# Stage borders, an affine step, and joined level pairs in a two-block transformer kernel on one core

## The reference

```python
# first block
h = x + stick_breaking(rms(x)) @ w_o;         h += swiglu(rms(h))
h += dilated(rms(h, mix), rms(h, kv)) @ w_o;  h += swiglu(rms(h));  h = rms(h, final)
# second block
h = layer_norm(ALPHA*h + hgrn2(h));           h = layer_norm(ALPHA*h + conv_ffn(h))
h = layer_norm(ALPHA*h + window(h, k, v));    h = layer_norm(ALPHA*h + conv_ffn(h))
# hgrn2, 8 heads:  S_t = diag(f_t) S_{t-1} + k_t v_t^T ;  o_t = S_t^T q_t
```

## Time and profile before

| | us |
|---|---|
| median of 3 runs (2432.78 to 2435.87) | 2432.88 |
| the profiled execution, its own time | 2434.52 |
| its span, first to last instruction | 2432.7 |
| PE busy | 2401.2 |
| DVE busy | 1430.5 |
| ACT busy | 909.2 |
| POOL busy | 162.3 |

### The profile page before, as it was taken

The page is one execution under the profiler, slowest core; times in us unless marked ns, Lnnn a source line. Parts: engine busy times, 40 slices in busy tenths (PEclk is TensorE's granted clock), DMA queues, the critical chain, the costliest instruction groups (busy, mean ns, idle before and its releaser), DMA issues.

```text
span 2432.7 us, 31033 instructions
## 1 busy us (share of the span) xinstructions
PE 2401.2 (99%) x11450; PEld 1958.9 (81%) x11450; DVE 1430.5 (59%) x2358; ACT 909.2 (37%) x1299; POOL 162.3 (7%) x171
## 2 busy tenths in 40 slices
PE   9999999999999999999989999999999999999998
PEld 7777888888777788888878887888888887888886
DVE  4776645533767555543278886766653766766643
ACT  4454322222756432222233333533321564433312
POOL 0000000000000000000020000000030451000031
PEclk9999999999999999999999999999999999999999
DMA  5122233233222233322231222233223412333232
GB/s 175 61 61 77 91 100 95 86 95 104 61 61 80 79 102 95 95 86 95 92 106 54 69 69 89 86 100 98 86 95 99 135 58 91 96 96 98 82 113 95
DMA packets 61078, 219.45 MB, mean 90 GB/s; under 512 B 6805, under 2 KB 7349, under 8 KB 60864
## 3 DMA queue, kind: packets, MB, share of 16 engines
q1 hardware_dynamic: 58464, 208.28, 27.0%
q0 software_dynamic: 2064, 9.50, 1.1%
q10 hardware_dynamic: 464, 0.48, 0.1%
HBM read 216.12 MB, written 2.12 MB: 90 GB/s over the span
## 4 chain that ended last, share of the span: by engine, by line
PE 93%; DVE 4%; ACT 2%; issue 1%; DMA 0%; DVEq 0%; SPq 0%; ACTq 0%
PE ps L264 26%; PE ps L266 26%; PE ps L265 26%; PE ps L2044 1%; PE ps L1066 1%; PE ps L303 1%; PE ps L304 1%; PE ps L308 1%; PE ps L1054 1%; PE ps L1223 1%; PE ps L1203 1%; PE ps L1080 1%; PE ps L1167 1%; PE ps L1168 1%; PE ps L1173 1%
## 5 line engine op out<-in xcount | busy, mean ns | idle before, releaser
L264 PE MATMUL ps<-xh,wh 128*128 128x512 f32 x1832 | 728.4, 398 | 5.2 <-DVE wl L258 5.2
L266 PE MATMUL ps<-xh,wl 128*128 128x512 f32 x1832 | 713.9, 390 | 0.0
L265 PE MATMUL ps<-xl,wh 128*128 128x512 f32 x1832 | 713.5, 389 | 0.0
L250 ACT ACTIVATE wh<-raw 128x1024 fp32r<-128x1024 f32 x331 | 348.1, 1055 | 509.7 <-PE ps L266 472.8
L258 DVE TENSOR_TENSOR wl<-raw,wh 128x1024 fp32r<-128x1024 f32 x331 | 409.0, 1237 | 203.4 <-ACT wh L250 201.7
L264 PEld LDWEIGHTS ps<-xh,wh 128*128 128x128 f32 x1832 | 344.2, 188 | 80.2 <-DVE wl L258 6.9
L266 PEld LDWEIGHTS ps<-xh,wl 128*128 128x128 f32 x1832 | 344.0, 188 | 72.5
L265 PEld LDWEIGHTS ps<-xl,wh 128*128 128x128 f32 x1832 | 344.4, 188 | 70.3 <-issue 2.2
L431 DVE TENSOR_TENSOR wl<-raw,wh 128x1024 fp32r<-128x1024 f32 x56 | 81.8, 1460 | 217.6 <-ACT wh L428 217.6
L264 PE MATMUL ps<-wh,up_ah 128*128 128x512 f32 x528 | 205.7, 390 | 1.1 <-DVE wl L431 1.1
L266 PE MATMUL ps<-wh,up_al 128*128 128x512 f32 x528 | 205.4, 389 | 0.0
(11 more groups left out here) (305 smaller groups left out, 3313.2 us busy)
## 6 DMA issues: line engine op xcount, KB each, us to landing
raw<-weights SPq DMA_DIRECT2D x387, 512.0 KB, 3.6
cst<-rows_d POOLq DMA_DIRECT2D x9, 512.0 KB, 5.0
hgrn_mask<-levels POOLq DMA_DIRECT2D x1, 2560.0 KB, 9.4
window_bias<-bias_rows POOLq DMA_DIRECT2D x1, 2048.0 KB, 10.1
hT<-x_t SPq DMA_DIRECT2D x7, 256.0 KB, 6.5
out_t<-hT SPq DMA_DIRECT2D x7, 256.0 KB, 2.1
cst<-consts SPq DMA_DIRECT2D x1, 832.0 KB, 9.0
raw<-weights SPq DMA_DIRECT2D x2, 256.0 KB, 4.5
```

Of the source, the lines that this page charges most:

```text
L250: act.activation(wh[slot][:, :], raw[slot][:, :], ACT.Copy).then_inc(hi_done, 1)
L264: pe.matmul(out, w_hi, m_hi, start=first, stop=False, **kw)
L265: pe.matmul(out, w_hi, m_lo, start=False, stop=False, **kw)
L266: return pe.matmul(out, w_lo, m_hi, start=False, stop=last, **kw)
```

## The change

- Recurrence: levels 6 and 7 become a fourth pair with a buffer `W3` and a mask more (11 levels in the mask table). Wide products alternate between two pairs of banks (0-1 and 2-3; in the last head 0-1 and 4-5). Seven products become six, ten picks eleven.
- POOL's gains of the norm behind down1 move from ahead of the recurrence into heads 1 to 4 of its loop, one tile in each, behind that head's root.
- Behind down1: squares of half 0 are taken as soon as that half is added; the second square covers 512 columns, and the root gets the first sum as a bias. DVE adds block b+1 before it normalises block b.
- Layer norms: both halves of the last block are normalised on DVE; tiles 0, 1, 2, 4 and 6 have their affine step on ACT, 3, 5 and 7 on DVE.
- Dilated border: the spread moves into the key projection, behind its fifth tile; the root and reciprocal stand behind the fourth tile of x2; ACT copies `rstd`; the split of slab 3 stands behind the cosine products.
- Tables: one dummy activation each for the root (behind up0), the exponential (ahead of the first head of dilated) and the root in the last hgrn head.
- down3: block 1 takes the third slab from the end right behind block 0. Two more warm-up matmuls at the start.

```diff
-PRODUCT_STEP = {1: 0, 5: 1, 9: 2, 13: 3, 16: 4, 18: 5, 20: 6}
+PRODUCT_STEP = {1: 0, 5: 1, 9: 2, 13: 3, 17: 4, 20: 5}
-WARM = 11
+WARM = 13
+        Y_DVE = (3, 5, 7)
...
+            ordered = [(k, b) for b in range(SB) for k in range(o.slabs - ends, o.slabs)]
+            if o.norm == "last":
+                ordered.insert(1, ordered.pop(ends))
...
+            if o.norm == "rms":
+                for b in range(SB):
+                    act.wait_ge(*o.added(b + 1))
+                    act.activation(residual[:, 2 * b, :], tokens(b, 0), ACT.Square,
+                                   accum_out=half_power[:, b:b + 1]).then_inc(o.stat.sem, 1)
...
+            if o.norm == "rms":
+                add(1, 0)
             for b in range(SB):
-                add(1, b)
+                if o.norm != "rms":
+                    add(1, b)
+                elif b + 1 < SB:
+                    add(1, b + 1)
...
-            project(pe, a.ph, 0, v_slab(0), ps[:, v_bank(0), :], a.x2h, a.x2l,
-                    between=lambda t: rms_pe_spread(pe, 2, 2) if t == 1 else None)
+            project(pe, a.ph, 0, k_slab(0), ps[:, k_bank(0), :], a.x2h, a.x2l, x_ready=(a.x2h_done, a.x2_ready, 0),
+                    between=lambda t: rms_pe_spread(pe, 2, 2) if t == 4 else None)
...
+            act.activation(small[:, 7:8], small[:, 0:1], ACT.Exp)
...
-            at = 2 if n == 1 and not tail else 0
+            at = (4 if tail else 2) * (n % 2)
...
             if attn:
+                dve_fill(dve, g, j, 6)
                 dve_uk(dve, g, j, 4)
                 dve_uk(dve, g, j, 5)
                 dve_pick_three(dve, g, j, 5, 2, 4, not proj)
...
                 dve_uk(dve, g, j, 6)
-                dve_uq(dve, g, j, 6)
-                dve_pick(dve, g, j, 8, 3, 6, 32, 0, not proj)
                 dve_uk(dve, g, j, 7)
-                dve_uq(dve, g, j, 7)
-                dve_pick(dve, g, j, 9, 4, 7, 64, 0, not proj)
+                dve_pick_three(dve, g, j, 8, 3, 6, not proj)
...
+            pool_head(pool, g, 0)
+            with pool.Fori(1, SB + 1) as j:
+                pool_head(pool, g, j)
+                pool.wait_ge(g.root_ready, j)
+                h = hT[:, bass.ds(2 * j - 2, 2), :].rearrange("p e s -> p (e s)")
+                pool.tensor_tensor(h, h, grow[:, :], ALU.mult).then_inc(o.affine.sem, 1)
...
-            rms_act_narrow(act, r_mix1, 3)
+                if j == 3:
+                    rms_act_narrow(act, r_mix1, 3)
+            act.wait_ge(spread_done.sem, 2)
+            act.activation(rstd[:, :], ps[:, 2, :], ACT.Copy).then_inc(r_mix1.rstd_ready, 1)
```

More of the change, by code:

```diff
@@ L625, in normed, with y_ready @@
                     return self.normed_act(1) if last and half else self.normed_dve(2 * b + half + 1)
-                return self.normed_dve(1) if last and not half else self.normed_act(2 * b + half + (not last))
+                return self.normed_dve(half + 1) if last else self.normed_act(2 * b + half + 1)
+            def y_ready(self, j):
+                if j in Y_DVE:
+                    return self.y_dve(Y_DVE.index(j) + 1)
+                return self.y_act(j + 1 - sum(n < j for n in Y_DVE))
             def bank_read(self, bank):
@@ L729, in tok_pe @@
                         turn_residual(1)
[L730 to L734, removed]
+            ordered = [(k, b) for b in range(SB) for k in range(o.slabs - ends, o.slabs)]
+            if o.norm == "last":
+                ordered.insert(1, ordered.pop(ends))
+            for k, b in ordered:
+                if b == 0:
+                    weights_ready(1, k)
+                part(1, k, b, b == SB - 1)
             if o.norm == "last":
@@ L771, in tok_act @@
             o.next_hi(act, 0)
+            if o.norm == "rms":
[3 more added lines that the diff above has]
+                                   accum_out=half_power[:, b:b + 1]).then_inc(o.stat.sem, 1)
+                act.wait_ge(*o.stat(SB))
+                act.activation(half_power[:, SB:2 * SB], half_power[:, 0:SB], ACT.Identity, scale=1.0 / D,
+                               bias=small[:, 0:1]).then_inc(o.stat.sem, 1)
             if o.norm == "last":
@@ L790, in tok_act @@
                     o.next_hi(act, 1)
-                if o.norm == "layer":
+                if o.norm == "layer" and b < SB - 1:
                     act.wait_ge(*o.shifted(b + 1))
-                    for half in range(b == SB - 1, 2):
+                    for half in range(2):
                         h = tokens(b, half)
@@ L813, in tok_act @@
                     y = (acc, rstd)[j % 2]
-                    if j % 2 == 0:
+                    if j not in Y_DVE:
                         act.wait_ge(*o.turned(j + 1))
@@ L894, in tok_dve @@
                     if b == SB - 1:
-                        h = tokens(b, 0)
-                        dve.tensor_scalar(h, h, mean, r, ALU.subtract, ALU.mult).then_inc(o.normed_dve.sem, 1)
+                        for half in range(2):
+                            h = tokens(b, half)
+                            dve.tensor_scalar(h, h, mean, r, ALU.subtract, ALU.mult).then_inc(o.normed_dve.sem, 1)
+                        continue
                     dve.tensor_scalar(power[:, b:b + 1], mean, r, -1.0, ALU.mult, ALU.mult).then_inc(o.shifted.sem, 1)
@@ L916, in tok_dve @@
             for j in range(KT):
[L917 to L926, removed]
+                if o.norm == "layer" and j + 1 in Y_DVE:
+                    dve.wait_ge(*o.turned(j + 2))
+                    dve.wait_ge(*o.x(j))
+                    dve.tensor_scalar(rstd[:, :], ps[:, o.banks[j + 1], :], gain(o.g, j + 1), gain(o.b, j + 1),
+                                      ALU.mult, ALU.add).then_inc(o.y_dve.sem, 1)
+                low(j)
             o.next_lo(dve, 2)
@@ L1978, in __init__ @@
                 self.F, self.vs, self.sig = (a(n, [P, S]) for n in ("F", "vs", "sig"))
-                self.W = [a(f"W{n}", [P, SB, 192]) for n in range(3)]
+                self.W = [a(f"W{n}", [P, SB, 192]) for n in range(4)]
                 self.G, self.v = a("G", [P, S]), a("v", [P, S])
@@ L2045, in pe_product @@
                                    start=b % 2 == 0, stop=True, skip_group_check=True)
[L2046 to L2055, removed]
+            elif n == 4:
                 for b in range(2):
-                    mm = pe.matmul(ps[:, 0 if tail else 2, token_block(b)], g.KG[:, token_block(2 * b)],
+                    mm = pe.matmul(ps[:, 0, token_block(b)], g.KG[:, token_block(2 * b)],
                                    g.QF[:, token_block(2 * b + 1)], start=True, stop=True)
@@ L2571, in _ @@
             up_act(act, up0)
+            act.activation(small[:, 7:8], small[:, 0:1], ACT.Sqrt)
             Out_then_rms(o_up0, r_mix1, up_sq).act(act)
```

103 lines of the change are left out of this document (52 added, 51 removed).

## The result

The changed kernel takes 2417.05 us (median of 4 runs, 2416.86 to 2417.28) against 2433.31 before (now four runs): 0.7% less, a ratio of 0.9931 with a 95% interval from 0.9914 to 0.9948. The forecast was 2415.1, with 2408 to 2426 as its range. On the scale of the profiled executions it was 2416.7; that of the changed kernel took 2417.28 for a span of 2415.5. So the sum of the terms is off by 0.6, and the rest of the 1.95 is the step to the median: the profiled execution of before lay 1.6 above its median, that of after 0.2.

What follows compares the result with a forecast made beforehand. PE's own stream was taken to set the time (busy 2401.2 of 2432.7 us); the terms summed to -17.8, taking the profiled 2434.5 to 2416.7, or 2415.1 on the median's scale, with a range from 2408 to 2426.

Steps and rivals of the forecast that it cites:

- POOL's tiles: Recurrence heads 1 to 4: POOL goes ahead of the `uq`, PE waits 1.05 us in each; +4.2 us.
- its nearest rival: Recurrence heads 1 to 4: POOL's tiles slip in behind the `uq` and cost nothing; 2410.9 us, chance 0.20.
- the finer point about the reciprocal: Recurrence heads with a POOL tile: a 512-column reciprocal beside POOL would be held too, as a 0.42 us instruction was.
- Joined pair: Recurrence, levels 6 and 7: one wide product replaces narrow ones, saving 0.67 us in each of eight heads; -5.4 us.
- The fourth product: Recurrence heads: needs `uk(5)`, placed 1.0 us ahead; a rival had it starve, slower from 2.2 us late, chance 0.06.
- Dilated: Border at the dilated stage: first three PE waits go and the last shrinks; -2.5 us, bounds -1.0 and -3.0.
- Behind down1: Border after down1: last transposes start sooner, -3.0 us; first half-clock stretch should not come, -1.0 us.
- the price of the clock: Behind down1: half of the 2 us that products share with the half-clock stretch; -1.0 us, bounds 0 and -1.7.
- First head: Recurrence's first head: without POOL's tiles the late splits are on time, -4.4 us; second half-clock stretch goes, -1.7 us.
- Last head and end: Last recurrence head: alternate banks remove waits for picks, -1.9 us; kernel end: block 1's matmuls cover a split, -1.2 us.
- Layer norms: Three layer norm borders: transposes no longer wait, second bank gives back 0.2 us; -0.3 us each, -0.9 us in all.
- Start: Kernel start: two more warm-up matmuls of about 0.11 us, covered by 1.4 us of PE standing still; term 0.

Runs made afterwards that it cites:

- pool_at_uq: The changed kernel with POOL's tile waiting for the last `uq` of the fill in place of the root; 2412.31 us, ratio 0.9904 to the kernel before.
- pairs_end_old: The changed kernel with levels 6 and 7 as separate products and the old order of down3's last slabs; 2423.73 us, ratio 0.9951 to the kernel before.
- rms_old: The changed kernel with only the border behind down1 set back (1024-column squares, next add behind the normalisation); 2422.36 us, ratio 0.9948 to the kernel before.
- pool_ahead: The changed kernel with POOL's four tiles ahead of the recurrence again; 2419.12 us, ratio 0.9932 to the kernel before.
- layer_old: The changed kernel with both layer norm edits set back (last half normalised on ACT, affine steps alternating); 2418.39 us, ratio 0.9928 to the kernel before.
- no_fetch: The changed kernel without the three dummy activations that fetch tables; 2418.95 us, ratio 0.9934 to the kernel before.

## Why the prediction was right, by its own steps

**POOL's tiles.** The step that made the difference between the forecast and its nearest rival held: POOL's tile starts 0.16 ahead of the last `uq`. Expected 1.05 a head, measured 1.20 (33.17 less 31.97). The second wide product starts 0.96 later against the first (1304.27 to 1309.27, against 1435.75 to 1439.79): the 0.80 of idle counts from the modelled end of the matmul before. The latency that the sum took as 0.15 is 0.06 here (`uk(1)` ends at 1309.21), so the slack is 1.23, and 2.2 less 1.23 gives 0.97. What is left, about 0.1 inside this product and 0.1 inside the fourth, the sum did not have. What was wrong is the finer point about the reciprocal: in pool_at_uq the tile starts 0.63 behind the start of that `uq`, 0.8 later than in the changed kernel, and is free, as the rival had it: the four heads take 4.8 less, where the rival said 4.2. How small a shift would do was not tried.

**Joined pair.** Forecast 0.67 a head, shown as 0.6 to 0.7 in the loop (pairs_end_old).

**The fourth product** did not starve. The margin I placed at 1.0 is 0.70 in a head without a tile (`uk(5)` ends at 1447.09, 0.06 of latency, product at 1447.85) and 0.13 in one with a tile (1317.31, product at 1317.50), where the product loses the 0.1 named above. The two `uk` stand in DVE's timeline as one row of 0.97:

```profile
1316.34 0.97 DVE L2247 TENSOR_TENSOR hgrn_KG<-hgrn_KG,hgrn_T 128x256 f32<-128x256 f32 x2
...
1446.12 0.97 DVE L2247 TENSOR_TENSOR hgrn_KG<-hgrn_KG,hgrn_T 128x256 f32<-128x256 f32 x2
```

**Borders.** Dilated: -2.6 for -2.5, with the new wait 0.91 for the 0.9 that the arrival at 639.0 and the readiness at 639.9 gave; but 0.9 of it hangs on the root's fetch together with the new order, which the sum did not part. Behind down1: -3.8 for -4.0, of which 3.2 lie ahead of the first product and the rest is the clock; the price of the clock holds for this trace only (rms_old). First head: -6.4 for -6.1, with both terms shown by pool_ahead. Last head and end: within 0.1. From the first wide product to the values the last head takes 18.63 (1467.74 to 1486.37) in place of 21.06; but the 2.2 that the sum called waits for picks show as 0.96 and 0.26 of idle in the trace of before, and what the other 1.0 was is not shown.

**Layer norms** is, by its share, the term that was most mis-sized: 0.5 in place of 0.9. By the starts of layer_old the last half on DVE brought 0.44 a border and not 0.5, and the second bank and what follows it gave 0.27 of it back and not 0.2.

**Start.** The term of nothing came out (-0.1), but not at the price named: the warm-up instructions begin 0.21 apart up to the last in the changed kernel, not 0.11, and the 1.4 of standing still is used up. No run takes this edit back.

**The sum** is nearer than its terms, which is luck in part: the loop's heads fell short by 0.5, the layer norms by 0.4 and the border behind down1 by 0.2, while the first head brought 0.3 more and 0.3 came at places for which nothing was forecast (start, up1, down1).

## What to carry to other kernels

What POOL's tile cost hung here on which DVE instruction stood next when it asked: 1.2 us a head ahead of the `uq`, nothing under the reciprocal. So find that instruction, and try to move the asking (here by 0.8 us) so that it falls under one that the trace shows not held. Where a stall at a border goes, look for a stretch of lowered clock behind it (0.50 for 3.41 to 6.83 us here) and count both, with a wide range for the second (0.7 to 1.6 here). Cost each table load (1.28 here) at the place where it stands, even between tiles that feed PE (0.9 of the root's load fell on PE in no_fetch).

## What was not expected of the hardware

A reciprocal of 128x512 (3.35) ran beside a POOL product of 128x1024 (2.40) with neither longer (pool_at_uq), while a product of 128x256 and a tensor_scalar of 128x512, 0.42 each, took 2.62 beside the same kind of tile (the changed kernel and the earlier trace rows). A standstill of 3.33 in pool_ahead, with the clock at 1.00 and a wait of 0.78 ahead of it, ended in a stretch at half clock that cost 1.6. And two waits of 1.04 and 1.68 went with 3.41 at half clock in one kernel and 6.83 in another.
